# Encoder trunk step on one Trainium2 core: TensorE without its dummy products around the first post-attention LayerNorm

## The chip, the cores and the metric

The kernel runs on one core of one Trainium2 chip. The metric is the device time of one execution in microseconds (us); lower is better. All times are of that one core.

## What is computed

One inference step of a streaming encoder trunk with one layer (width 1024), for 256 prompt frames and 64 sample frames, so 320 tokens that share all weights. Cut to what matters here:

```python
def trunk_layer(x, p, ...):
    z = x @ w_in                                   # 1024 -> 4608
    q, k, v, u, vs, ga, gb = jnp.split(z, SPLIT_POINTS, axis=-1)
    oa = chunk_attention(q, k, v, rel_table)       # prompt or sample form
    un, vn = gelu(u), layer_norm(gelu(vs), mlp_ln_g, mlp_ln_b)
    ob = spatial_gating(un, vn, mlp_w_s, mlp_b_s)
    mix = sigmoid(ga) * (oa @ w_branch_a) + sigmoid(gb) * (ob @ w_branch_b)
    x = layer_norm(ALPHA * x + mix @ w_out, ln1_g, ln1_b)      # the first norm after attention
    ff = moe_ffn(x, ...)        # sigmoid router, 64 experts, top 8, plus one shared expert
    x = layer_norm(ALPHA * x + ff, ln2_g, ln2_b)
    return x + sigmoid(x @ ple_w_gate) * (p @ ple_w_proj)
```

## The kernel before, in words

The 320 tokens lie in three row tiles of 128, 128 and 64 rows. All of it is one program written by hand, one instruction stream per engine, ordered by semaphores: TensorE (PE) multiplies and transposes, ScalarE (ACT) and VectorE (DVE) move results out of PSUM and do the pointwise work, GpSimd (POOL) helps, SyncE (SP) issues the DMAs. Large products are made from split operands: every fp32 weight and activation is cut into a high and a low fp32r half, and high\*high, high\*low and low\*high are summed, so each 128x128 weight tile costs three products with 320 columns (`products`, line 1341).

In order of time the program is: input norm and its transposes, the projection `w_in` in 36 column tiles, attention and gating, the branch products, the product with `w_out` (8 tiles, line 1341), **the first norm after attention**, the router, the shared expert and the top-8 choice, a loop over the 64 experts in steps of four (weights streamed by DMA into `expert_ring`), the second norm, the gate and the output.

The place of the change, engine by engine:

- PE turns the eight `w_out` result tiles back to rows (line 1493), and then waits on `residual` until DVE has added the residual for all three row tiles (line 1082, three instructions).
- DVE then runs the norm alone: statistics (L885, L889), variance (L891), the square root on ACT (L623), and for each row tile a centring pass (L895) and a scaling pass (L905). Each scaled tile raises `ln_done`.
- PE meanwhile issues `keep_warm(WARM[1], 7)`: 24 products of the identity with itself into PSUM bank 7, a bank that no one reads then (line 1315). In the trace each such fp32 product shows as two matrix instructions, so 24 products are 48 rows. The rows of the whole program count 100: 32 of the 16 products at the start (`WARM[0]`), 48 and 20 here.
- For each row tile PE waits for `ln_done` and makes eight transposes of it (`transpose_rows`, line 1307). ACT copies each turned tile out of PSUM as the high half (L646), DVE subtracts to get the low half (L938) and raises `x1T_ready`.
- PE issues `keep_warm(WARM[2], 7)`, 10 products (20 rows), then waits for `router_low` (POOL, L583) and for all three `x1T_ready`, and makes the 24 router products (line 1507). Then follow the shared expert's products (line 1341 again), which end with the mask of the top-8 choice in between (L1531, L1533), and its second product (line 1559).

```python
            pe.wait_ge(residual, 3)
            keep_warm(WARM[1], 7)
            for t in range(3):
                pe.wait_ge(ln_done, 7 + t)
                transpose_rows(xs, t, 2 * t, x1T_ps)

            keep_warm(WARM[2], 7)
            pe.wait_ge(router_low, 1)
            pe.wait_ge(x1T_ready, 3)
```

The dummy products wait for nothing and nothing waits for them but what stands behind them in PE's own stream.

Of the kernel before, what the change touches and what calls it, by code (L numbers as in the profile page):

```python
# [46 lines left out]
def trunk_step(nc, x_prompt, x_sample, cache_k, cache_v, p_prompt, p_sample, ln_in_g, ln_in_b, w_in,  # L47
# [30 lines left out]
    with ExitStack() as ctx:  # L78
# [279 lines left out]
        PLE_BANK = (7, 4, 2, 3, 4, 2, 3, 4)  # L358
        MEAN_BANK, VAR_BANK = 5, 6

        WARM = (16, 24, 10)
        GATE_GROUPS = ((0, 4), (4, 6), (6, 8))
        SCAT_BANK = (2, 3, 7, 0, 1, 3, 7, 0)
        AHEAD = 5
# [938 lines left out]
        def _(pe):  # L1303
# [7 lines left out]
            def keep_warm(n, bank):  # L1311


                for _ in range(n):
                    pe.matmul(PS[:, bank, 0:P], ident[:, :], ident[:, :], start=True, stop=True)  # L1315

            pe.wait_ge(const_ready, 1)
            pe.wait_ge(var_ready, 1)
            keep_warm(WARM[0], 7)
            for t in range(3):  # L1320
                pe.wait_ge(ln_done, t + 1)
                transpose_rows(xs, t, 2 * t, xT_ps)
# [170 lines left out]
                    ins = pe.transpose(PS[0:ROWS[t], (4, 6, 0)[t] + j // 4, P * (j % 4):P * (j % 4 + 1)], woT[:, j, cols(t)], ident[:, :])  # L1493
                ins.then_inc(out_ps, 1)
            pe.wait_ge(residual, 3)
            keep_warm(WARM[1], 7)
            for t in range(3):
                pe.wait_ge(ln_done, 7 + t)
                transpose_rows(xs, t, 2 * t, x1T_ps)

            keep_warm(WARM[2], 7)
            pe.wait_ge(router_low, 1)
            pe.wait_ge(x1T_ready, 3)
            for k in range(KD):
# [278 lines left out]
```

## Time and profile before

| what | value |
|---|---|
| median of 3 timed runs | 895.85 us (900.4, 895.85, 888.97) |
| the profiled execution, its own time | 891.24 us |
| its span, first to last instruction | 889.5 us |
| PE busy | 830.3 us, 93% of the span, 5015 products |
| DVE busy | 388.4 us, 44% |
| ACT busy | 265.9 us, 30% |
| mean granted TensorE clock | 0.979 |

The span is the time between the first and the last instruction that the profile shows; the execution's own time is 1.74 us longer. The granted clock is the share of TensorE's full clock that its throttle let through: 1.00 is 2.4 GHz and 0.50 is 1.2 GHz, and a stretch in which it changes shows a mean of the two. A busy PE is a PE with at least one product in flight, not one at full speed: what a product costs in a row of products is the length of the row by their number.

### The profile page before, as it was taken

The page shows a single profiled execution, that of the slowest core. Times are in us where ns is not written, and L with a number is a line of the kernel's source. Part 1 is how long each engine was busy: PE and PEld are TensorE (multiplying, and loading weights), DVE is VectorE, ACT ScalarE, POOL GpSimd, SP SyncE. Part 2 cuts the span into 40 slices and gives each one's busy share as a digit, 9 for nine tenths or more (in the row PEclk, how much of TensorE's full clock was granted, in tenths as well). Part 3 has the DMA queues.
Part 4 walks back from the last instruction along what each step waited for, and adds up shares of the span by engine and source line. Part 5 has one row for each costly group of instructions (what it writes and reads, how often), then busy time and mean ns, then how long its engine had stood idle before and what let it go on. Part 6 is the DMA issues. An engine that isn't in the chain of part 4 may idle for free.

```text
span 889.5 us, 13632 instructions
## 1 busy us (share of the span) xinstructions
PE 830.3 (93%) x5015; PEld 573.9 (65%) x5015; DVE 388.4 (44%) x845; ACT 265.9 (30%) x499; POOL 44.6 (5%) x57
## 2 busy tenths in 40 slices
PE   4999899889989799999999999999999999979887
PEld 3899799879988545554654645555464464543577
DVE  7343575747468824224314413422431441340574
ACT  2244466733423412211211221221121022021453
POOL 3200100000002300000000000000000000000300
PEclk9999999989999999999999999999999999999999
DMA  9744424417790059999999999999999999995001
GB/s 306 200 163 160 157 97 141 160 49 280 293 381 6 1 198 424 380 389 384 426 384 383 424 387 386 424 381 386 384 424 389 381 424 387 385 421 195 1 1 60
DMA packets 66043, 249.03 MB, mean 280 GB/s; under 512 B 5856, under 2 KB 37040, under 8 KB 41440
## 3 DMA queue, kind: packets, MB, share of 16 engines
q1 hardware_dynamic: 64848, 244.70, 69.7%
q0 software_dynamic: 1152, 3.95, 1.6%
q8 instruction: 17, 0.28, 0.1%
q14 instruction: 10, 0.08, 0.0%
q10 hardware_dynamic: 16, 0.02, 0.0%
HBM read 245.62 MB, written 3.03 MB: 280 GB/s over the span
## 4 chain that ended last, share of the span: by engine, by line
PE 84%; DVE 8%; DMA 3%; ACT 2%; issue 2%; SPq 0%; ACTq 0%; DVEq 0%; PEldq 0%
PE PS L1578 25%; PE PS L1341 20%; PE PS L1594 13%; PE PS L1608 9%; PE PS L1543 9%; PE PS L1718 3%; DMA weight_ring<-in_w_in_dram 2%; DVE xs L905 1%; DMA weight_ring<-in_shared_w_dram 1%; PE PS L1587 1%; DVE xs L895 1%; DMA expert_ring<-in_ln_in_b_dram 1%; PE PS L1551 1%; DVE z L1181 1%; DVE parts L1176 1%
## 5 line engine op out<-in xcount | busy, mean ns | idle before, releaser
L1578 PE MATMUL PS<-expert_ring,z 128*64 128x512 f32 x1024 | 227.1, 601 | 6.5 <-issue 6.5
L1341 PE MATMUL PS<-parts,split 128*128 128x320 f32 x1344 | 201.8, 312 | 7.0 <-DVE parts L1060 3.3
L1341 PEld LDWEIGHTS PS<-parts,split 128*128 128x128 f32 x1344 | 199.9, 190 | 8.2 <-PEq L1483 3.5
L1578 PEld LDWEIGHTS PS<-expert_ring,z 128*64 128x64 f32 x1024 | 72.6, 138 | 147.8 <-issue 147.5
L1594 PE MATMUL PS<-expert_ring,z 128*64 128x512 f32 x512 | 113.7, 596 | 0.0
L931 DVE TENSOR_TENSOR split<-weight_ring,split 128x512 fp32r<-128x512 f32 x106 | 72.5, 692 | 92.6 <-ACT split L634 92.3
L1216 DVE TENSOR_TENSOR split<-PS,split 128x512 fp32r<-128x512 f32 x64 | 44.3, 692 | 142.9 <-ACT split L777 142.4
L634 ACT ACTIVATE split<-weight_ring 128x512 fp32r<-128x512 f32 x112 | 69.7, 630 | 116.2 <-PE PS L1341 98.5
L1203 DVE SCALAR_TENSOR_TENSOR z<-PS,z 128x256 f32<-128x256 f32 x32 | 15.5, 485 | 190.8 <-ACT z L768 190.8
L768 ACT ACTIVATE z<-PS 128x256 f32<-128x256 f32 x32 | 12.3, 384 | 284.7 <-PE PS L1578 284.7
L1543 PEld LDWEIGHTS PS<-marks,parts 128*128 128x128 f32 x640 | 78.7, 191 | 14.5 <-issue 14.3
L1543 PE MATMUL PS<-marks,parts 128*128 128x256 f32 x640 | 85.0, 287 | 0.0
L1608 PEld LDWEIGHTS PS<-marks,split 128*128 128x128 f32 x512 | 75.2, 188 | 14.0 <-issue 13.0
L1608 PE MATMUL PS<-marks,split 128*128 128x320 f32 x512 | 80.4, 314 | 0.0
L1594 PEld LDWEIGHTS PS<-expert_ring,z 128*64 128x64 f32 x512 | 34.6, 136 | 65.7 <-issue 65.4
L777 ACT ACTIVATE split<-PS 128x512 fp32r<-128x512 f32 x64 | 38.3, 598 | 80.6 <-PE PS L1594 80.6
L1220 DVE TENSOR_TENSOR z<-z,PS 128x320 f32<-128x320 f32 x128 | 54.3, 484 | 11.7 <-PE PS L1608 10.1
L753 ACT ACTIVATE z<-PS 128x512 f32<-128x512 f32 x64 | 38.2, 597 | 55.5 <-PE PS L1543 55.5
L1718 PE MATMUL PS<-parts,split 128*128 128x320 f32 x192 | 30.9, 322 | 3.5 <-ACT expert_ring L855 1.9
L1718 PEld LDWEIGHTS PS<-parts,split 128*128 128x128 f32 x192 | 29.7, 198 | 4.4 <-issue 4.2
L602 POOL TENSOR_TENSOR expert_ring<-z 128x320 f32<-128x320 f32 x1 | 0.9, 873 | 517.4 <-DVE z L1220 517.4
L1315 PE MATMUL PS<-ident 128*128 128x128 f32 x100 | 15.0, 321 | 11.2 <-DVE vareps L891 9.4
(232 smaller groups left out, 571.5 us busy)
## 6 DMA issues: line engine op xcount, KB each, us to landing
expert_ring<-in_exp_w_dram SPq DMA_DIRECT2D x192, 1024.0 KB, 10.0
weight_ring<-in_w_in_dram SPq DMA_DIRECT2D x36, 512.0 KB, 4.3
weight_ring<-in_w_out_dram SPq DMA_DIRECT2D x8, 512.0 KB, 4.5
expert_ring<-in_ple_w_gate_dram SPq DMA_DIRECT2D x2, 2048.0 KB, 10.3
weight_ring<-in_w_branch_a_dram SPq DMA_DIRECT2D x4, 512.0 KB, 3.4
weight_ring<-in_w_branch_b_dram SPq DMA_DIRECT2D x4, 512.0 KB, 4.6
weight_ring<-in_shared_w_dram SPq DMA_DIRECT2D x4, 512.0 KB, 8.2
xs<-in_x_prompt_dram SPq DMA_DIRECT2D x2, 512.0 KB, 4.2
```

The costliest lines, as they stand in the source:

```text
L634: nc.scalar.activation(split[:, 2 * (place % 2) + half, 0, :].rearrange("p (k n) -> p k n", k=4), raw, ACT.Copy)\
L753: nc.scalar.activation(xgT[:, 2 * g:2 * g + 2, :].rearrange("p k s -> p (k s)"), PS[:, g % 2, :], ACT.Copy)\
L777: nc.scalar.activation(ysplit[:, j, 0, 512 * half:512 * half + 512], PS[:, 5 + half, :], ACT.Copy)\
L931: nc.vector.tensor_tensor(parts[:, 1, :, :], raw, parts[:, 0, :, :].bitcast(F32), ALU.subtract).then_inc(w_low, 1)
L1216: nc.vector.tensor_tensor(ysplit[:, j, 1, c], PS[:, 5 + half, :], ysplit[:, j, 0, c].bitcast(F32), ALU.subtract).then_inc(y_low, 1)
L1220: nc.vector.tensor_tensor(accT[:, q, :], accT[:, q, :], PS[:, SCAT_BANK[q], 0:TOK], ALU.add)\
L1341: ins = pe.matmul(out, w[:, wp, :], xT[:, xp, k0 + k, :], start=(start and k == 0 and (wp, xp) == (0, 0)), stop=(stop and k == 3 and wp == 1))
L1543: ins = pe.matmul(PS[:, g % 2, 256 * k:256 * k + 256], xrows[:, part, t, 2 * g + k, :], pick[:, t, :], start=(t == 0 and part == 0), stop= ...
L1578: ins = pe.matmul(PS[c, 2 + j, :], xgT[:, k, P * j + 64 * e:P * j + 64 * e + 64], w13(j, e, k), start=(k == 0), stop=(k == KD - 1))
L1594: ins = pe.matmul(PS[c, 5 + half, :], hidT[:, j, k, c], w2(j, e, k, half), start=(k == 0), stop=(k == 1))
L1608: ins = pe.matmul(PS[:, SCAT_BANK[q], 0:TOK], ysplit[:, j, part, P * q:P * (q + 1)], scat[:, j, 0:TOK], start=(j == 0 and part == 0), stop ...
L1718: ins = pe.matmul(PS[:, tile % 2, 0:TOK], w[:, wp, :], xT[:, xp, k, :], start=(k == 0 and (wp, xp) == (0, 0)), stop=(k == KD - 1 and wp == 1))
```

## The change

The two calls of `keep_warm` around the norm go, with their 24 and 10 products. The 16 products at the start of the program stay. No other instruction is added, removed or moved, on PE or on any other engine.

```diff
-        WARM = (16, 24, 10)
+        WARM = 16
...
-            keep_warm(WARM[0], 7)
+            keep_warm(WARM, 7)
...
             pe.wait_ge(residual, 3)
-            keep_warm(WARM[1], 7)
             for t in range(3):
                 pe.wait_ge(ln_done, 7 + t)
                 transpose_rows(xs, t, 2 * t, x1T_ps)
 
-            keep_warm(WARM[2], 7)
             pe.wait_ge(router_low, 1)
             pe.wait_ge(x1T_ready, 3)
             for k in range(KD):
```

## Rows read from the trace of the kernel before

**Rows 1.** The page: the span, and the granted clock in 40 slices.
```profile
span 889.5 us, 13632 instructions
...
PEclk9999999989999999999999999999999999999999
```

**Rows 2.** The chain that ended last, 250 to 320 us: start, length, what.
```profile
272.77 2.43 PE PS L1315 x20
275.20 3.58 PE PS L1507 x24
```

**Rows 3.** Timeline, 255 to 300 us: start, length, engine, line, count, [idle before <- releaser].
```profile
255.91 2.84 PE L1493 MATMUL PS<-ident,z 128*128 128x128 f32 x24 [1.82 <-ACT z L723]
...
260.57 7.25 PE L1315 MATMUL PS<-ident 128*128 128x128 f32 x48 [1.82 <-DVE xs L1082]
...
268.48 1.09 PE L1307 MATMUL PS<-ident,xs 128*128 128x128 f32 x8 [0.66 <-DVE xs L905]
...
270.86 1.90 PE L1307 MATMUL PS<-ident,xs 128*128 128x128 f32 x16 [1.29 <-DVE xs L905]
271.93 2.94 DVE L938 TENSOR_TENSOR parts<-PS,parts 128x1024 fp32r<-128x1024 f32 x3
...
272.70 2.50 PE L1315 MATMUL PS<-ident 128*128 128x128 f32 x20
...
275.02 3.76 PE L1507 MATMUL PS<-parts,marks 128*128 128x320 f32 x24
```

**Rows 4.** Instructions on the tile parts, 268 to 276 us: ns min/median/max.
```profile
L646 ACT ACTIVATE parts<-PS x3: 590/1024/1024, 269.6 to 272.9; 128x1024 fp32r<-128x1024 f32 x2, 128x512 fp32r<-128x512 f32 x1
L938 DVE TENSOR_TENSOR parts<-PS,parts x3: 680/1208/1214, 271.9 to 274.2; 128x1024 fp32r<-128x1024 f32 x2, 128x512 fp32r<-128x512 f32 x1
```

**Rows 5.** Stretches of 2 us, PE alone: length, PE busy (count), PEclk, DMA share, GB/s.
```profile
26.00:28.00 2.00, 2.00 (x15) 0.98 1.09 301
...
186.00:188.00 2.00, 2.00 (x27) 0.88 0.00 0
...
226.00:228.00 2.00, 2.00 (x11) 0.64 1.11 395
...
260.00:262.00 2.00, 1.43 (x11) 0.90 1.01 422
...
264.00:266.00 2.00, 2.00 (x16) 0.75 1.00 406
...
316.00:318.00 2.00, 2.00 (x16) 0.95 0.61 213
...
862.00:864.00 2.00, 2.00 (x14) 0.92 0.00 0
```

**Rows 6.** Timeline, PE alone: where its work began again after a wait.
```profile
23.30 15.58 PE L1341 MATMUL PS<-parts,split 128*128 128x320 f32 x96 [0.21 <-issue]
...
180.56 0.70 PE L1450 MATMUL PS<-expert_ring 128*64 128x128 f32 x4 [1.07 <-DVE expert_ring L1042]
...
224.24 29.85 PE L1341 MATMUL PS<-parts,split 128*128 128x320 f32 x192 [3.26 <-DVE parts L1060]
...
312.69 0.59 PE L1551 MATMUL PS<-z 128*128 128x10 bf16 x6 [5.04 <-DVE z L1157]
...
858.91 12.34 PE L1718 MATMUL PS<-parts,split 128*128 128x320 f32 x72 [1.94 <-ACT expert_ring L855]
```

**Rows 7.** Timeline, PE alone, 20 to 23 us: transposes while the clock was low.
```profile
20.00 1.11 PE L1307 MATMUL PS<-ident,xs 64*128 64x64 f32 x8 [1.12 <-DVE xs L905]
21.12 1.97 PE L1327 MATMUL PS<-ident,expert_ring 128*128 128x128 f32 x8
```

**Rows 8.** Timeline, PE alone: 192 branch products at the full clock throughout.
```profile
192.56 28.42 PE L1341 MATMUL PS<-parts,split 128*128 128x320 f32 x192 [1.49 <-PEq L1473]
```

**Rows 9.** Stretches: PE, PEld, DVE, ACT, POOL busy (count), PEclk, DMA share, GB/s.
```profile
261.60:265.00 3.40, 3.40 (x19) 3.40 (x18) 3.33 (x10) 0.18 (x1) 0.00 (x0) 0.50 1.00 416
...
275.00:307.00 32.00, 30.17 (x182) 26.41 (x182) 24.94 (x128) 14.56 (x20) 9.45 (x7) 1.00 0.00 1
```

## The prediction

> **What bounds the kernel now.** I read the page first, then the chain of waits around the norm, then the timeline of that stage on all engines, and last the granted clock in short stretches. The page shows a kernel of 889.5 us whose TensorE is at its full clock almost everywhere [rows 1]; one slice in 40 is lower. Of the whole span the change touches only what lies between 258.8 and 275.2 us, where PE has nothing real to do but 24 transposes. The reader should see three things there.
>
> First, the norm is DVE's. PE's last real work ends at 258.75 (255.91 + 2.84), the first transpose starts at 268.48 and the second group at 270.86, each released by the scaling pass L905 [rows 3]. The 48 rows of dummies fill 260.57 to 267.82 and stand 0.66 us clear of that release, so the first removed call delays nobody.
>
> Second, the chain of waits names the second call as a link of its own: 2.43 us of L1315 right before the router's products [rows 2]. That is only half the picture. DVE's low halves L938 run beside it, 271.93 to 274.87, and the router needs them [rows 3]. The router began at 275.02; without the dummies it could have begun at about 274.9. A link in the chain is worth no more than the lead it has over the next one, and here that lead is some 0.1 us.
>
> Third, the clock. PE's short pause before the dummies was enough for it to fall: the stretch 260 to 262 has a mean of 0.90, so it fell at about 261.6 (0.5 for 0.4 us of the 2), and 264 to 266 has 0.75, so it was back at 265.0 [rows 5]. All of that low time, 3.4 us at 0.50, lay under dummy products [rows 9]. The transposes after them have full-clock lengths, and from 275 to 307 us, the router included, the clock was 1.00 [rows 9]. So the dummies take no time on the path, and what they give is that real work finds the full clock.
>
> **The change, part by part.**
>
> *The 24 products go.* The gain on the path is 0, for the reason above. PE is then idle from 258.75 to 268.48, 9.7 us in one piece. The longest idle pieces that the rows show elsewhere are 5.04 and 3.26 us, and behind both the clock was at 0.50 when work began again [rows 5, 6]. I therefore take it that the transposes start at 1.2 GHz.
>
> What do slow transposes cost? Eight of a 128-row tile take 1.09 us at the full clock [rows 3] and took 1.97 us at the low one; eight of the 64-row tile took 1.11 us there [rows 7]. The first tile has slack: its low half waits for DVE, which is busy scaling until about 272. The second decides: it starts at 270.86 as before (DVE sets that), ends at 272.83, ACT's high half takes 1.02 us to about 273.9, DVE's low half 1.21 us to 275.1; the third tile's last transpose comes at 273.94, its high half (0.59) at 274.6, and its low half (0.68) behind the second's at 275.8 [rows 4]. Against 274.87 that is +0.9 us, and against the router's start of 275.02 it is +0.85, with what the second call had in lead already in it. Bounds: 0 if the clock came back before 270.9, and 1.2 us if ACT and DVE add their usual small gaps on each hand-over.
>
> *The 10 products go.* Gain 0.1 us at most, and it is spent in the line above: the path that waits now is the low halves. So I enter 0 for it.
>
> *Low clock under the router and the shared expert.* From about 275.9 PE runs without a break, and the clock will come back some time into that row of products. Six rises in this trace bound how long. I take the rise from the mean in the 2 us stretch [rows 5] and the start from the row in which PE's work began [rows 6], or for the dummies [rows 3]: 23.30 to 26.1, 180.56 to 186.5, 224.24 to 227.4, 260.57 to 265.0, 312.69 to 316.2 and 858.91 to 862.3. The delays are 2.8, 5.9, 3.2, 4.4, 3.5 and 3.4 us, mean 3.9. The price of a low microsecond comes from the same 192 products twice: 28.42 us at the full clock [rows 8], and 29.85 us with the first 3.2 us low [rows 6], so 1.43 us for 3.2 us, or 0.45 per us. The term is 0.45 x 3.9 = +1.75 us, between 0.45 x 2.8 = 1.25 and 0.45 x 5.9 = 2.65.
>
> The Trainium skill, page "TensorE: Matmul & The Clock Gate", section "Terms", prices throttled time at one minus the clock share, which is 0.50 per low microsecond where the rows say 0.45; by it this term would be 1.95 and the whole sum about +2.8. The measured rows decide, and nothing below uses the page's figure.
>
> *What hides it?* Nothing. PE is without idle time from 275.02 to 294.3, and DVE's top-8 choice and ACT's row copies wait for PE's products before and after it. PE is busy 30.17 of the 32 us from 275 to 307 [rows 9]. The expert weights are already in place by then (the DMA share of that stretch is 0.00), so no load can absorb a shift either. I count the delay in full.
>
> *Later places.* PE waits again before the expert loop, and the clock is low for 3.5 us from 312.69 and for 3.4 us from 858.91. A shift of some 2.5 us can move these a little either way, from 2.8 to 5.9 us of low time in place of about 3.4, so -0.3 to +1.1 us each. I enter 0 and keep the ends for the range.
>
> **Sum.** 0.85 + 0 + 1.75 = +2.6 us, so the profiled execution's 891.24 (span 889.5 and 1.74 around it) would become 893.8. The own bounds are +1.2 (no delay before the router, 1.25 under it) and +3.9 (1.2 and 2.65), or up to +6 with both later places against it. The profiled execution is 4.6 us below the median shown, and the four times known (888.97, 891.24, 895.85, 900.4) have their middle at 893.55. I set the sum on that middle: 893.55 + 2.6 = 896.2 us. Differences under 2% (18 us) are about what a measurement of this kernel can't tell from no change, and this sum is 0.3%.
>
> **The rivals.**
>
> *The chain was right and the dummies cost.* Then the 2.43 us of rows 2 come back and the clock does no harm: 893.55 - 2.4 = 891.1. For it speaks the chain, against it L938's end at 274.87, 0.15 us ahead of the router's start.
>
> *The clock comes back during the transposes.* Then the router starts at the full clock and only some of the 0.85 is paid, say +0.4: 894.0. For it: the transposes make PE busy for 4 to 5 us. Against it: the transposes from 20.00 to 23.09 ran at the low clock to the end, and the clock rose only at 26.1, in the products behind them [rows 5 to 7].
>
> *The clock stays low through the whole routing stage, slower by over 2%.* The place is 275 to 307 us. Its 30.17 us of work would take 30.17 / 0.55 = 54.9 us at the low clock; the 1.8 us of idle time taken off, that is +23 us, and with the 0.85 before it 893.55 + 23.8 = 917.4. It is over 2% from some 38 us of low time on (17 / 0.45). For it: the attention stage, whose work comes in short pieces with waits between, was still low 5.9 us after its work had begun again. Against it: no unbroken row of products stayed low for more than 5.9 us, and this one is unbroken for 19 us. The Trainium skill's section "A second HAM failure mode: psum-queue depth-cycling" on the same page tells of a kernel whose many short pauses sent the clock up and down; here the trace of before shows 1.00 from 275 to 307, with 1.8 us of pauses in it, which speaks against that.
>
> **How the numbers follow.** The forecast has 0.70, the clock back in the transposes 0.14, the chain's gain 0.08, the long low stage 0.03, and 0.05 is for what I don't see, on either side. All but the third rival lie within 2%, so faster by over 2% has 0.02, within 2% 0.94 and slower 0.04. The runs of before spread more than the effect: the range goes from the lowest run with no loss (889.0) to the highest with the sum on it (900.4 + 2.6 = 903.0).
>
> **What would show it right or wrong.** In the profile after, L1315 should have 32 rows in place of 100, PE one idle piece of 9 to 10 us before the first transpose, ended by L905 with the norm's passes as long as before. The stretch from 262 to 275 should be at 0.50, eight transposes at about 2.0 us, the last L938 about 0.9 us later after L905 than now, and the clock should return 2.8 to 5.9 us into the router's products; low time grows by some 14.5 us (265.0 to about 279.8), so the mean clock falls from 0.979 to about 0.971. The forecast is wrong if the clock is 1.00 at the first transpose, if the router starts more than 0.3 us earlier after the last L905 than now, or if 0.50 lasts beyond 283 us.

## The result, and the profile after

The changed kernel is slightly faster, not slower: 889.27 us against 895.18 us (medians of 19 runs each), a ratio of 0.9939 with a 95% interval of 0.9918 to 0.9961. The forecast was +2.6 us; measured were -5.5 us (-3.5 to -7.3). The size is within the 2% that was named, the sign is wrong. The absolute time lies just inside the stated range (889.0 to 903.0), but by luck: the range's lower end was the fastest run of before with no loss added.

First the norm, in the timeline of the changed kernel (columns as in [rows 3]).

```profile
255.77 2.84 PE L1493 MATMUL PS<-ident,z 128*128 128x128 f32 x24 [2.16 <-ACT z L723]
...
268.43 1.94 PE L1307 MATMUL PS<-ident,xs 128*128 128x128 f32 x8 [9.82 <-DVE xs L905]
...
270.72 3.01 PE L1307 MATMUL PS<-ident,xs 128*128 128x128 f32 x16 [0.35 <-DVE xs L905]
...
275.75 6.42 PE L1505 MATMUL PS<-parts,marks 128*128 128x320 f32 x24 [2.02 <-DVE parts L938]
...
282.01 1.92 PE L1341 MATMUL PS<-parts,split 128*128 128x320 f32 x12
...
316.18 0.60 PE L1549 MATMUL PS<-z 128*128 128x10 bf16 x6 [5.14 <-DVE z L1157]
```

Beside [rows 3]: PE waits 9.82 us in one piece, eight transposes take 1.94 us in place of 1.09, the router's products start 0.73 us later although the stage began 0.14 us earlier, and 24 of them take 6.42 us in place of 3.76. The granted clock of the same stretches (columns as in [rows 5]) says why:

```profile
260.00:262.00 2.00, 0.00 (x0) 0.80 1.04 434
262.00:264.00 2.00, 0.00 (x0) 0.50 0.97 399
...
276.00:278.00 2.00, 2.00 (x8) 0.50 0.00 0
...
280.00:282.00 2.00, 2.00 (x10) 0.58 0.00 0
282.00:284.00 2.00, 2.00 (x16) 1.00 0.00 0
```

The clock is low from 261.2 to 281.7 us; in the kernel before it was back at 265.0 [rows 5]. So around the norm the change costs what was forecast and somewhat more: the shared expert's products begin at 282.01 where they began at 278.62, and the first expert step at 316.18, 3.49 us later than in [rows 6].

Where, then, does the gain come from? The timeline of the expert loop's end gives it. The kernel before, columns as above:

```profile
788.90 5.03 PE L1608 MATMUL PS<-marks,split 128*128 128x320 f32 x32
800.45 15.85 PE L1578 MATMUL PS<-expert_ring,z 128*64 128x512 f32 x64 [6.52 <-issue]
826.41 5.02 PE L1608 MATMUL PS<-marks,split 128*128 128x320 f32 x32
...
872.31 7.29 PE L1718 MATMUL PS<-parts,split 128*128 128x320 f32 x48
```

And the changed kernel, where the same lines are two lower:

```profile
793.70 5.03 PE L1606 MATMUL PS<-marks,split 128*128 128x320 f32 x32
799.42 13.95 PE L1576 MATMUL PS<-expert_ring,z 128*64 128x512 f32 x64 [0.69 <-DVE z L1220]
823.49 5.04 PE L1606 MATMUL PS<-marks,split 128*128 128x320 f32 x32
...
855.99 10.80 PE L1716 MATMUL PS<-parts,split 128*128 128x320 f32 x72 [1.95 <-ACT expert_ring L855]
867.85 7.29 PE L1716 MATMUL PS<-parts,split 128*128 128x320 f32 x48
```

The changed kernel arrives at the loop's end 4.80 us late (793.70 against 788.90). Then the kernel before waits 6.52 us for "issue", that is for nothing that the profile shows, and comes out of it with the clock down, so that the 64 rows of products (two for each fp32 product) take 15.85 us. The changed one waits 0.69 us for DVE and takes 13.95 us. The clock of that stretch (columns as in [rows 5]), in the kernel before and then in the changed one:

```profile
800.45:817.00 16.55, 16.55 (x70) 0.88 0.40 148
```

```profile
800.45:817.00 16.55, 16.49 (x81) 1.00 0.87 341
```

At the next row of the two timelines the changed kernel is 2.92 us ahead. The remaining 1.54 us come from the gate: 10.80 us against the 12.34 of [rows 6], because in this execution the clock did not fall there. That can't be put down to the change: of the thirteen profiles of this document, five show 12.33 or 12.34 us for these 72 products and eight show 10.79 or 10.80, with and without dummies on either side. Together, for the whole span: +4.80 - 5.83 - 1.89 - 1.54 = -4.5 us, the difference of the spans (885.0 and 889.5 us).

The 5.83 us that fell away leave a trace in the DMA queues of that stretch, 794 to 801 us. The queue view of the kernel before (queue, kind: packets, MB, share of 16 engines):

```profile
q8 instruction: 2, 0.03, 1.8%
```

In the changed kernel the two fetches of instructions come in 801 to 810 us, while PE is at work:

```profile
q8 instruction: 2, 0.03, 1.4%
```

That is not later as seen from the loop's end. In shorter stretches of the same view the first of the two comes at 797.5 us in the kernel before and at 802.3 us in the changed one, both 8.6 us after the start of the loop's last 32 products (L1608, L1606). So both kernels make the fetch. In the kernel before PE stands still until 2.9 us after it; in the changed one PE had gone on 2.9 us before it. The view doesn't name the engine that a queue serves; that q8 is PE's is inferred from these times.

Behind the loop the program reads the number of further rounds and branches over the code of a second loop, which these inputs don't need (`more > 0` at L1690 of the kernel before). PE's last step lies behind that branch. The theory (F): in the kernel before PE has to wait for the fetch of the code it needs next, in the changed one it has that code already, because all code behind the norm lies 135 instructions earlier. The profiles count 13632 and 13497 instructions. The rival (D): what helps is that the dummies themselves are gone.

### The profile page after: what moved, and what is told of

It reads as the page before. It is cut to its first block, busy times and chain, and to the rows that moved or that the text cites. A ratio compares the mean times of both kernels' runs of the same rounds, so it can differ in the third digit from the quotient of the medians.

```text
span 885.0 us, 13497 instructions
## 1 busy us (share of the span) xinstructions
PE 825.1 (93%) x4947; PEld 570.1 (64%) x4947; DVE 388.2 (44%) x845; ACT 266.2 (30%) x499; POOL 44.3 (5%) x57
## 4 chain that ended last, share of the span: by engine, by line
PE 83%; DVE 8%; DMA 3%; ACT 2%; SPq 1%; issue 1%; ACTq 0%; DVEq 0%; PEldq 0%
PE PS L1576 25%; PE PS L1341 19%; PE PS L1592 13%; PE PS L1606 9%; PE PS L1541 9%; PE PS L1716 2%; DMA weight_ring<-in_w_in_dram 2%; DMA weight_ring<-in_shared_w_dram 1%; DVE xs L905 1%; PE PS L1585 1%; DVE xs L895 1%; PE PS L1549 1%; DVE z L1181 1%; DMA expert_ring<-in_ln_in_b_dram 1%; PE PS L1505 1%
## 5 line engine op out<-in xcount | busy, mean ns | idle before, releaser
L1606 PEld LDWEIGHTS PS<-marks,split 128*128 128x128 f32 x512 | 75.2, 188 | 14.0 <-issue 13.0
L1606 PE MATMUL PS<-marks,split 128*128 128x320 f32 x512 | 80.5, 314 | 0.0
L1157 DVE TENSOR_TENSOR marks<-z 128x256 fp32r<-128x256 f32 x51 | 18.6, 420 | 9.2 <-PE PS L1541 8.8
```

Source lines behind the costliest of these rows:

```text
L1606: ins = pe.matmul(PS[:, SCAT_BANK[q], 0:TOK], ysplit[:, j, part, P * q:P * (q + 1)], scat[:, j, 0:TOK], start=(j == 0 and part == 0), stop ...
```

## The experiments

All ratios are to runs of the kernel before on the same chip, with 95% intervals; 1% is 8.9 us.

**Put the code back where it was, without the dummies.** The changed kernel with

```diff
+        padding = sem("padding")
...
+            for _ in range(135):
+                pe.sem_inc(padding, 1)
             pe.wait_ge(residual, 3)
```

> The changed kernel with 135 semaphore increments that nobody waits for put on PE ahead of its wait for the residual, where it idles 9.8 us; they make PE's instruction stream as long ahead of the expert loop as it was in the kernel before, without any dummy product. Theory F (the gain is an instruction fetch that PE no longer waits for when it leaves the expert loop, because the code behind it lies elsewhere by 135 instructions): the idle time of 6 to 7 us, put down to issue, is back in front of the first product of the last expert step, and only the loss at the norm is left of the change, so 1.004 to 1.006 of the time of before (+3.4 to +5 us). Theory D (what helps is that the dummy products themselves are gone, by the clock or by another timing of the loop's end): no such idle time, 0.992 to 0.996 of before, as the changed kernel.

Measured: 1.0113 (1.0076 to 1.0150). The increments weren't hidden; the first row shows 18.6 us of them before the transposes, 8.8 more than the changed kernel idles there. The idle time behind the loop is back in full:

```profile
277.60 4.69 PE L1308 MATMUL PS<-ident,xs 128*128 128x128 f32 x24 [18.60 <-issue]
...
812.60 16.75 PE L1579 MATMUL PS<-expert_ring,z 128*64 128x512 f32 x64 [6.42 <-issue]
```

The wait goes with the place of the code, not with the dummies. The time itself is blurred by the price of the padding.

**Move the code on by 121, with all dummies.** The kernel before with

```diff
+        padding = sem("padding")
...
+                    for _ in range(121):
+                        pe.sem_inc(padding, 1)
                     pe.wait_ge(pick_bf_ready, 3)
```

> The kernel before, all dummies in place, with 121 semaphore increments that nobody waits for on PE, in its 5 us wait ahead of the first expert step; 121 is 256 less 135, so if code is fetched in pieces of 256 instructions (one fetch in the trace is 16 KB), the code behind the loop lies in its piece where the changed kernel has it. Theory F: the 6.5 us of idle time goes and the clock stays up behind it (13.95 in place of 15.85 us for that step's 64 products), with no loss at the norm: -7 to -8 us, 0.991 to 0.993 of before. Theory D: 0.998 to 1.003, the idle time stays.

Measured: 1.0028 (0.9998 to 1.0058). Here too the padding showed, 16.16 us where 5.04 us of waiting were to be had, so 11.1 us on the path. But the wait behind the loop went; the first fetch of q8 comes 8.8 us after the start of the loop's last products (8.6 in the kernel before), and here PE is at work by then:

```profile
326.19 0.58 PE L1552 MATMUL PS<-z 128*128 128x10 bf16 x6 [16.16 <-issue]
...
808.70 13.95 PE L1579 MATMUL PS<-expert_ring,z 128*64 128x512 f32 x64 [0.70 <-DVE z L1221]
```

+2.5 us measured less 11.1 for the padding is -8.6, near the forecast of -7 to -8. Both expectations had the trace right and the price of an increment wrong: it is 0.13 to 0.14 us (18.60 / 135, 16.16 / 121). A loss at the norm stands in this trace too, with all dummies in place:

```profile
260.70 5.62 PE L1316 MATMUL PS<-ident 128*128 128x128 f32 x48 [1.82 <-DVE xs L1083]
...
271.00 3.01 PE L1308 MATMUL PS<-ident,xs 128*128 128x128 f32 x16 [1.29 <-DVE xs L906]
...
277.40 3.77 PE L1508 MATMUL PS<-parts,marks 128*128 128x320 f32 x24
```

The 24 dummies ran at the full clock (5.62 us in place of 7.25), and then the clock fell to 0.50 at 269.7 us, as the first group of transposes ended; the other two groups took 3.01 us in place of 1.90.

**The same two with padding that is never executed.** The increments stand under a condition that is false for these inputs, at the same wait:

```diff
+        padding = sem("padding")
...
+                    spare = pe.value_load(rounds_i[0:1, 0:1], min_val=0, max_val=MAX_ROUNDS - 1)
+                    with pe.If(spare > 0):
+                        for _ in range(117):
+                            pe.sem_inc(padding, 1)
                     pe.wait_ge(pick_bf_ready, 3)
```

(131 in place of 117 in the changed kernel).

> The kernel before with a branch, in PE's 5 us wait ahead of the first expert step, over 117 semaphore increments that are never executed for these inputs; with the four instructions of the branch PE's code behind it lies 121 instructions later, as with the 121 executed increments, without their 16 us. Theory F (fetch behind the expert loop): no idle time of 6 us after the loop, 0.990 to 0.993 of before, that is -6.5 to -8.5 us, if the branch itself stays hidden in the wait. Theory D (the dummies themselves): 0.999 to 1.003.

Measured: 0.9912 (0.9880 to 0.9944), -7.9 us.

> The changed kernel with such a branch over 131 increments that are never executed, so the code behind lies 135 instructions later than in the changed kernel, where the kernel before has it. Theory F: the 6.5 us of idle time is back and the loss at the norm stands alone: 1.002 to 1.006 of before (+2.5 to +5 us). Theory D: 0.992 to 0.996.

Measured: 1.0042 (1.0014 to 1.0071), +3.8 us. The row behind the loop in the one with the dummies, then in the one without:

```profile
795.71 13.95 PE L1579 MATMUL PS<-expert_ring,z 128*64 128x512 f32 x64 [0.49 <-DVE z L1221]
```

```profile
800.88 16.42 PE L1577 MATMUL PS<-expert_ring,z 128*64 128x512 f32 x64 [6.23 <-issue]
```

This is the clean pair: with the code in one place the change is faster by 5.5 us, with the code back in its old place slower by 3.8. Theory D falls. (The second of the two kernels has one branch more than the kernel before; the next experiment shows that such a branch costs nothing that its interval shows.)

**Half the distance.** The same branch over 60 increments, a shift of 64.

> The kernel before with the branch over 60 increments that are never executed, so the code behind lies 64 instructions later in place of 121. Theory F: the idle time is either there in full or gone, nothing between; 64 later lies halfway between a place that has it (0) and one that has not (121), so both are open: 0.999 to 1.002 with it, 0.990 to 0.993 without. A rival to F, that the branch ahead of the loop or its reading of the count helps by itself and not the place of the code: 0.990 to 0.993 and no idle time whatever the length.

Measured: 0.9979 (0.9945 to 1.0012), with the wait in full:

```profile
804.17 16.87 PE L1579 MATMUL PS<-expert_ring,z 128*64 128x512 f32 x64 [6.22 <-issue]
```

So neither the extra branch nor its reading of the count helps; the length does.

**Without the branch behind the loop.** PE falls through to the last step:

```diff
-            more = pe.value_load(rounds_i[0:1, 0:1], min_val=0, max_val=MAX_ROUNDS - 1)
-            with pe.If(more > 0):
...
-            expert_step(more * STEPS + STEPS - 1, None, last=True)
+            expert_step(STEPS - 1, None, last=True)
```

> The kernel before without PE's conditional rounds behind the expert loop (these inputs need none): PE reads no count, takes no branch over the second loop's code and falls through to the last step. It leaves out the further rounds that PE would make for other inputs. Theory F: what PE waits for is code that lies behind a taken branch, so the 6.5 us of idle time goes, -6 to -8.5 us, 0.990 to 0.993 of before. Theory D: 0.998 to 1.002.

> The changed kernel without PE's conditional rounds behind the loop (these inputs need none, other inputs would), to stand beside the kernel before without them (0.989). Neither takes the branch, so what is left between the two is what the dummies do around the norm. Theory F with the prediction's local terms: +2.5 to +5 us, 0.992 to 0.995 of before, no idle time behind the loop, the clock low from some 3 us into the norm until 3 to 6 us into the router's products. Theory D: not slower than 0.989.

Measured: 0.9892 (0.9854 to 0.9931) with the dummies and 0.9919 (0.9888 to 0.9950) without. Neither waits behind the loop; the row for both, with the dummies first:

```profile
800.38 13.96 PE L1578 MATMUL PS<-expert_ring,z 128*64 128x512 f32 x64
```

```profile
800.36 13.95 PE L1576 MATMUL PS<-expert_ring,z 128*64 128x512 f32 x64
```

Of the two fetches of q8 at the loop's end the first is gone in both kernels, the second in the one without dummies. This fits code behind a taken branch as what is waited for; the edit also takes the skipped code out, so it doesn't tell the branch from the distance that it skips. What is left between the two, +2.4 us, has the sign and size that the dummies' removal should have, but the intervals overlap, so by itself it isn't shown. The changed kernel against the one with skipped padding, both without the wait, gives +2.4 us as well (0.9939 - 0.9912), again with intervals that overlap. The changed kernel with the code put back gives +3.8 with an interval clear of 0.

**Each half of the change alone.** Without the 24 (`keep_warm(WARM[1], 7)` taken out), a shift of 95:

> The first half of the change alone: the 24 dummies go, the 10 stay; PE's code ahead of the expert loop is 95 instructions shorter. Around the norm: idle for 9.8 us and the clock low there, as in the changed kernel, but up a little sooner in the router's products because of the 10 (+1.5 to +3.5 us). Behind the loop, theory F says only that the idle time is either there in full (6 to 7 us) or gone; of the shifts tried 0 has it and some 120 and 135 shorter have not, and 95 is nearer to those, so I expect it gone: 0.992 to 0.996. If it is there: 1.002 to 1.004.

Measured: 0.9934 (0.9904 to 0.9965). The wait in full is gone, but a short one stands in the middle of the step's products, which I had said there could not be:

```profile
802.77 4.50 PE L1577 MATMUL PS<-expert_ring,z 128*64 128x512 f32 x19 [0.73 <-DVE z L1220]
808.01 10.03 PE L1577 MATMUL PS<-expert_ring,z 128*64 128x512 f32 x45 [0.74 <-issue]
```

PE ran the first 19 of the 64 rows from code that was there, and then waited for the rest, until 2.4 us after the first fetch of q8 (805.6 us). Around the norm this kernel did as expected: the transposes ran at the low clock, the 10 dummies took 3.97 us in place of 2.50 and the clock came back under them, so the router ran at the full clock (3.77 us). It began 2.5 us later than in the kernel before, both counted from the stage's start.

Without the 10 (`keep_warm(WARM[2], 7)` taken out), a shift of 40, and the same with 40 executed increments that put the code back:

> The second half of the change alone, with nothing to make up for its 40 instructions. Around the norm no change (-0.1 to 0 us). Behind the loop the code is 40 instructions earlier, nearer to the place that has the idle time: I expect it there, 0.998 to 1.002; if it is gone, 0.990 to 0.993.

> The kernel before without the 10 dummies ahead of the router alone, with 40 increments in the wait ahead of the first expert step so that the code behind lies where it did. By the terms of the prediction: the router starts 0 to 0.1 us earlier, and the clock stays at 1.00, because PE idles only some 2 us between the last transpose and the router: 0.999 to 1.001. A rival: that pause is enough for the clock to fall in some executions, up to +1.7 us (1.002).

Measured: 1.0006 (0.9978 to 1.0034) and 1.0012 (0.9982 to 1.0041); both keep the wait of 6.4 to 6.5 us behind the loop. Around the router my expectation failed in the trace: with all 24 dummies in place, the clock falls behind the pause that the 10 had filled. The second of the two kernels, timeline and stretches:

```profile
277.62 5.30 PE L1507 MATMUL PS<-parts,marks 128*128 128x320 f32 x24 [2.25 <-DVE parts L939]
```

```profile
276.00:278.00 2.00, 0.38 (x3) 1.00 0.00 0
278.00:280.00 2.00, 2.00 (x9) 0.51 0.04 8
280.00:282.00 2.00, 2.00 (x10) 0.64 0.00 0
```

The router took 5.30 us against 3.76 [rows 3]. So the 10 are not idle decoration: they cover a wait of 2.25 us behind which, 0.4 us into the router's products, the clock was at 0.50. In the time that is 1.5 us here, which these intervals can't tell from none. The first of the two kernels can't be read in this way: there the clock had fallen before this pause, at 274.1 us, by the end of the first group of transposes, and the router took 5.48 us.

**The dummies kept, their code short.** Both rows of dummies made by loops of one product:

```diff
-            keep_warm(WARM[1], 7)
+            with pe.Fori(0, WARM[1]):
+                keep_warm(1, 7)
...
-            keep_warm(WARM[2], 7)
+            with pe.Fori(0, WARM[2]):
+                keep_warm(1, 7)
```

> The kernel before with its 24 and its 10 dummies each made by a loop on PE of one product, so that all dummy work stays and PE's code ahead of the expert loop is some 120 instructions shorter. Theory F: near the 135 of the change, so the idle time behind the loop should go, 0.990 to 0.994 of before, with the clock up at the router; a loop of dummies may end 1 to 2 us later than the straight row. Theory D: 0.999 to 1.004.

Measured: 0.9922 (0.9895 to 0.9950), no wait for issue behind the loop, all dummy work in place:

```profile
264.29 9.71 PE L1315 MATMUL PS<-ident 128*128 128x128 f32 x48 [1.89 <-DVE xs L1082]
273.83 2.58 PE L1307 MATMUL PS<-ident,xs 128*128 128x128 f32 x24
276.34 3.60 PE L1315 MATMUL PS<-ident 128*128 128x128 f32 x20
279.82 3.75 PE L1509 MATMUL PS<-parts,marks 128*128 128x320 f32 x24
...
800.47 13.95 PE L1580 MATMUL PS<-expert_ring,z 128*64 128x512 f32 x64 [0.73 <-DVE z L1220]
```

The loop stretches the 24 dummies from 7.25 to 9.71 us, so that the first transposes no longer find PE waiting, but the router runs at the full clock. By their ratios this kernel, the one with the skipped padding (0.9912) and the two without the branch are all ahead of the changed one, by 1.5 to 4.2 us with intervals that overlap. The one with the skipped padding keeps the dummies, handles further rounds as the kernel before does, and has the best ratio of those that leave nothing out, by less than the intervals can tell.

## Why the prediction went wrong

**The norm: right for the execution that was read.** The first removed call delayed nobody, and PE's idle piece was 9.82 us (forecast 9.7). The clock was low at the transposes, eight of them took 1.94 us (forecast 1.97), and the router started 0.73 us later, 0.87 measured from the stage's own start (forecast 0.85). But that with the dummies real work finds the full clock was read from one execution. Of the five profiles of kernels with both rows of dummies straight in the code, two show the clock fall among the transposes: the one with 121 increments, shown above, and the one without the branch (2.82 us for the 16 rows). From the stage's start to the end of the router's products it took 22.87 us in the kernel before, 25.13 and 25.77 in these two, and 26.40 in the changed kernel. So in a trace the loss is 3.5 us or as little as 0.6, by the execution that it is set against.

**The low clock under the router: right in kind, at the top of its bounds.** The clock rose at 281.7 us, 5.9 us into the products (bounds 2.8 to 5.9, entered 3.9). At 0.45 us each that is 2.65; the 24 products grew by 6.42 - 3.76 = 2.66 us. One of the six rises was misread: PE had worked at the low clock since 20.00 us [rows 7], not since 23.30, so the 2.8 us are no delay from the start of its work; the other five have a mean of 4.1. The mean clock fell from 0.979 to 0.972 (forecast 0.971), an agreement that is in part chance, since the low time that went behind the loop and at the gate was not in that sum.

**Later places: the step that failed.** The prediction entered 0 for everything behind the norm but a shift of the clock's low stretches, from -0.3 to +1.1 us each. One of these was there: the first expert step stayed low longer, +1.31 us up to its scatter (4.80 - 3.49). The other went, -1.54 us. Neither is shown to be the change's: the kernel with a shift of 64, all dummies in place, has as slow a first step (its first two rows of products 3.68 and 2.50 us, the changed kernel 3.68 and 2.47, the kernel before 3.40 and 1.45), and the gate goes either way, as told above. But the term that set the sign was missing: leaving the expert loop, where 5.83 us of waiting and 1.89 us of low clock fell away. That no other instruction is moved was true of the order, not of where the instructions lie, and I had not looked at the loop's end at all, because the change doesn't touch it. The row was on the first page of the profile of before, in its list of the costliest groups:

```profile
L1578 PE MATMUL PS<-expert_ring,z 128*64 128x512 f32 x1024 | 227.1, 601 | 6.5 <-issue 6.5
```

6.5 us in one wait on an engine that is 93% busy, put down to nothing that the profile shows, is a question that should have been asked. The prediction gives 5.04 and 3.26 us as the longest idle pieces that its rows show, and this one was not among the rows. An answer was at hand: the Trainium skill, page "Runtime: NRT & Kernel Launch", section "Instruction fetch mechanics", says that instructions are fetched in blocks of 16 KiB, 256 instructions, and that a taken branch to a target outside the two blocks at hand has to wait until its block is fetched. The runs agree as far as they go: two fetches made 0.03 MB, and with shifts of -135 and +121, which differ by 256, there was no wait. Which blocks PE holds at the branch, no run here shows. With that section the change would have had a rival "code behind the loop moves by 135", with a price of some 6 to 8 us if it moves out of the wait.

**The rivals.** None of those named came true. The chain's 2.43 us for the second call was no gain, as said: in the kernel without it the router waits for L938 in the same place. The clock didn't come back during the transposes, and the long low stage did not occur. The three signs that the prediction gave for being wrong (the clock at the first transpose, the router's start, the end of the low clock) all lie around the norm, and none of them came true; no sign watched the place that decided.

**The sum as it should have been.** +2.4 us (the pair without the branch) to +3.8 us (the code put back) around the norm, -7.9 us behind the loop (the kernel with all dummies and skipped padding), together -4.1 to -5.5; measured -5.5 (-3.5 to -7.3). The +2.4 us of the changed kernel against the skipped padding can't check this sum, being the measured -5.5 less that -7.9.

## What to carry to other kernels

Removing or adding instructions on an engine moves all its code behind them, and where a branch skips far ahead, that alone can open or close a wait of several microseconds; a gain of half a percent from an edit is not shown to be the edit's until the same edit has been tried with the code behind it held in place. Any wait that the profile puts down to issue on the engine that bounds the kernel should be looked up in the instruction queue's rows before a prediction is made. Whether dummies keep a clock up should be read from more than one execution: here they did so in three of five. A loop makes their code short and a pad under a false condition moves the code behind them, and the length is then chosen by the wait behind the next long branch.

## What was not expected of the hardware

- The fetch wait had about one size wherever it stood in full, 6.2 to 6.5 us in six of the kernels here, and it also costs the clock: the 64 rows of products behind it took 15.85 to 16.87 us in place of 13.95.
- In all eleven kernels that keep the branch, with the wait or without it, the first fetch came 8.3 to 8.8 us after the start of the loop's last products. In the six with the wait in full PE went on 2.9 us after that fetch, in four it had gone on 2.8 to 3.0 us before it, and in the one with a part it stood still from 1.7 to 2.4 us after it.
- By shift of PE's code ahead of the loop, in instructions: full wait at -40, 0 and +64, a part of 0.74 us at -95, none at about -120, at -135 and at +121.
- A semaphore increment on PE takes 0.13 to 0.14 us, so 121 to 135 of them are no free padding.
- Behind a pause of 2.25 us after 24 transposes the clock was at half speed 0.4 us after the router began, in the profile shown above.
